# A hybrid attention and state-space trunk on one core: the two state-space stages become one, and the scanned states are laid by step, part and group

## What is computed

```python
proj = hn @ w_in;  u, z = proj[..., :1024], proj[..., 1024:]      # 64 groups of 16 channels
# per group, per direction, 64 complex states h:
#   h[t] = A * h[t-1] + B u[t],   y[t] = Re(C h[t])               (diagonal A)
y = (y_fwd + y_bwd) + d * u
gl = gelu(y);  y = gl * sigmoid(gl @ w_glu + b_glu);  y = y * silu(z)
return y @ w_out
```

## Time and profile before

| what | us |
|---|---|
| median of 3 runs (2629.58 to 2637.1) | 2631.95 |
| the profiled execution, its own time | 2628.88 |
| its span in the trace | 2627.0 |
| PE busy | 2325.1 |
| DVE busy | 1185.6 |
| ACT busy | 886.2 |
| POOL busy | 841.2 |

### The profile page before, as it was taken

How to read it: one execution, slowest core, us unless ns; L and a number is a source line. 1 busy time by engine, 2 the same in 40 slices (tenths; PEclk the granted TensorE clock), 3 DMA queues, 4 the chain that set the end, 5 groups by cost and what they waited for, 6 DMA issues and landing times. The chain is left out here.

```text
span 2627.0 us, 38336 instructions
## 1 busy us (share of the span) xinstructions
PE 2325.1 (89%) x13896; PEld 1865.8 (71%) x13896; DVE 1185.6 (45%) x2668; ACT 886.2 (34%) x2256; POOL 841.2 (32%) x1283
## 2 busy tenths in 40 slices
PE   4999999999999999999999999398799980558888
PEld 3777777777777777777777777277788760457767
DVE  5242443443353353353353353343325999435434
ACT  4233434333433433333333333232433210133221
POOL 1715655555565465466111111010111110211200
PEclk9999999999999999999999999599899995778989
DMA  4212221322222222222221220254554420874333
GB/s 143 60 51 61 60 80 51 84 74 56 74 67 73 66 75 73 66 83 65 64 63 45 47 63 21 65 185 155 202 169 150 144 93 0 213 208 154 136 138 120
DMA packets 191828, 249.69 MB, mean 95 GB/s; under 512 B 86176, under 2 KB 140320, under 8 KB 189472
## 3 DMA queue, kind: packets, MB, share of 16 engines
q1 hardware_dynamic: 191648, 247.30, 31.8%
HBM read 153.23 MB, written 62.55 MB: 82 GB/s over the span
## 5 line engine op out<-in xcount | busy, mean ns | idle before, releaser
L1066 PE MATMUL att_pj<-hT_hi,att_wh 128*128 128x512 f32 (+1 forms) x1920 | 710.0, 370 | 10.8 <-DVE att_wl L848 10.8
L1066 PE MATMUL att_pj<-hT_hi,att_wl 128*128 128x512 f32 (+1 forms) x1920 | 683.8, 356 | 0.0
L1066 PE MATMUL att_pj<-hT_lo,att_wh 128*128 128x512 f32 (+1 forms) x1920 | 682.7, 356 | 0.0
L704 POOL TENSOR_TENSOR att_sw<-att_sw,att_rope 128x1280 f32<-128x1280 f32 x48 | 201.5, 4198 | 762.9 <-DMA att_sw<-att_t 762.8
L1066 PEld LDWEIGHTS att_pj<-hT_hi,att_wh 128*128 128x128 f32 x1920 | 364.5, 190 | 58.5 <-DVE att_wl L848 11.4
L860 DVE CUSTOM_DVE_ANT_0 att_sm<-att_sc,att_mask 128x128 f32<-128x128 f32 (+2 forms) x480 | 152.4, 355 | 561.6 <-PE att_sc L982 560.4
L1066 PEld LDWEIGHTS att_pj<-hT_hi,att_wl 128*128 128x128 f32 x1920 | 363.6, 189 | 53.0
L1066 PEld LDWEIGHTS att_pj<-hT_lo,att_wh 128*128 128x128 f32 x1920 | 364.9, 190 | 45.5
L730 ACT ACTIVATE att_pr<-att_sm,att_stats 128x128 f32<-128x128 f32 (+2 forms) x480 | 215.0, 449 | 434.1 <-PE att_tr L992 313.0
L772 ACT COPY att_t<-att_pj 128x512 f32<-128x512 f32 (+1 forms) x216 | 111.3, 515 | 377.9 <-PE att_pj L1066 377.7
L879 DVE TENSOR_TENSOR att_t<-att_t,att_rope 128x1280 f32<-128x1280 f32 x48 | 71.8, 1495 | 201.8 <-DMA att_sw<-att_t 201.8
(11 more groups left out here) (224 smaller groups left out, 3835.7 us busy)
## 6 DMA issues: line engine op xcount, KB each, us to landing
att_raw<-in_w_att_dram SPq DMA_DIRECT2D x80, 512.0 KB, 3.8
att_sw<-att_t SPq DMA_DIRECT2D x192, 160.0 KB, 2.9
f_scratch<-att_ft SPq DMA_DIRECT2D x32, 256.0 KB, 2.3
e_scratch<-att_place SPq DMA_DIRECT2D x8, 1024.0 KB, 4.6
front_raw<-in_w_ssm_dram SPq DMA_DIRECT2D x16, 512.0 KB, 6.4
front_f<-f_scratch SPq DMA_DIRECT2D x16, 512.0 KB, 5.1
front_f<-e_scratch SPq DMA_DIRECT2D x16, 512.0 KB, 3.6
back_e<-e_scratch SPq DMA_DIRECT2D x8, 1024.0 KB, 7.5
```

Of the source, the lines that this page charges most:

```text
L704: pool.tensor_tensor(sw[:], sw[:], rope[:, 1], ALU.mult).then_inc(sin_done, 1)
L1066: last = pe.matmul(pj[:, c % 3, 0:n], w[:, k % 2, kt], h[:, kt, lo:lo + n], start=(r == 0), stop=(r == CHUNK_MMS - 1))
```

## The change

- The two stages become one (`ssm_stage`): no stage end stands between scan and back part. The SBUF of the front's weights and inputs is used again for the back part's matrices: the near matrices of all 64 groups at once (`near`), `e` in seven buffers, u and y in two. All eight PSUM banks serve the back part.
- The back part goes by 24 joints of 3, 3 and 2 groups per batch; the groups of a joint share a PSUM bank and one gelu. The near products of eight joints are made first (`near_part`); then, per joint, the two products with the entering states, and the near products of the joint seven ahead.
- Loads for the back part are issued when PE has finished the front's products, in the order near (8 transfers of 192 KB), u of two batches, two e, near (16 transfers), five e, then u of the third batch once the near products of the first are made.
- The forward half of the entering states is copied by ACT (`entering`) in place of POOL, the backward half still by DVE.
- `st` is laid by chunk, part, group: a scan step's 128 elements lie side by side, and one group's chunks 128 floats apart. `dec`, `t1`, `t2` follow. There is no zero column any more: column n holds the state that enters chunk n, so that the last chunk's leaving state is dropped and the scan has 31 and 96 steps.
- `leaving` of tile n-1 stands between c1 and c2 of tile n, where it stood after c2. ACT copies a group's forward half with one instruction of 318 elements, where it used two of 256 and 64; DVE's two become 254 and 62.

The core of the diff:

```diff
-        st = held.enter_context(nc.sbuf_tensor("states", [P, SG, 2, SCOLS], F32))
+        st = m.sb("states", [P, NC, 2, SG])
+        states = st[:].rearrange("p n r g -> p g r n")
...
+        e = m.sb("e", [P, E_BUFS, 2, GB, L * SC])
+        near = m.sb("near", [P, SG, P])
...
+            def u_again(b):
+                if b >= 2:
+                    sp.wait_ge(local, PARTS * (b - 1))
+                sp.dma_start(u2[:, b % 2], u_scratch[b].rearrange("s c g n -> (s c) g n")).then_inc(u2_in[b % 2], 16)
...
             sp.wait_ge(k_stored, 16 * HALVES)
+            sp.wait_ge(done, 3 * NT)
+            near_load(0)
+            u_again(0)
+            u_again(1)
+            for b in range(2):
+                e_load(b)
+            near_load(1)
+            near_load(2)
+            for b in range(2, E_BUFS):
+                e_load(b)
+            sp.wait_ge(stored, U_STORED)
+            u_again(2)
+            u_again(3)
...
+                    if c == len(CHUNKS) - 1 and 1 <= n <= NB:
+                        for g in range(GB * (n - 1), GB * n):
+                            act.wait_ge(left, g + 1)
+                            act.copy(states[0:64, g, :, 1:NC], part(g, slice(0, 64))[:, :, 0:NC - 1]).then_inc(fwd, 1)
                     act.wait_ge(done, 3 * n + c + 1)
...
+            def entering(j):
+                if j >= 2:
+                    act.wait_ge(y_done, j - 1)
+                g = joint_groups(j)
+                act.copy(en[0:64, j % 2, 0:len(g)], states[0:64, g[0]:g[-1] + 1]).then_inc(enter_f, 1)
...
-                prev = st[:, :, :, bass.ds(c, n, step=PC + 1)]
-                cur = st[:, :, :, bass.ds(c + 1, n, step=PC + 1)]
+                prev = st[:, bass.ds(c, n, step=PC)]
+                cur = st[:, bass.ds(c + 1, n, step=PC)]
...
                 for c, (lo, cnt) in enumerate(CHUNKS):
+                    if c == len(CHUNKS) - 1 and 1 <= n <= NB:
+                        leaving(n - 1)
...
-                if 1 <= n <= NB:
-                    leaving(n - 1)
...
+            for j in range(BANKS):
+                near_part(j)
+            for j in range(JOINTS):
+                b = j // PARTS
+                if j % PARTS == 0:
+                    pe.wait_ge(e_in[b], 16)
+                pe.wait_ge(enter_f, j + 1)
+                pe.wait_ge(enter_b, 2 * (j + 1))
...
+                last.then_inc(y_done, 1)
+                if j >= 1 and j - 1 + BANKS < JOINTS:
+                    pe.wait_ge(y_out, j)
+                    near_part(j - 1 + BANKS)
```

More of the change, by code:

```diff
@@ L59 @@
 NB = SG // GB
-SCOLS = NC + 2
 TWO_PI = 6.283185307179586
@@ L1279, with joint_groups, ssm_stage @@
 TAPS = 2 * L - 1
[L1282 to L1283 removed]
+BANKS = 8
+PART = 3
+PARTS = -(-GB // PART)
+JOINTS = NB * PARTS
+def joint_groups(j):
+    b, i = divmod(j, PARTS)
+    return list(range(GB * b + PART * i, min(GB * b + PART * (i + 1), GB * (b + 1))))
+def ssm_stage(nc, w_d, h_scratch, skip_d, f_scratch, e_scratch, bb_scratch, c0_scratch, decay_scratch,
+              u_scratch, z_scratch, kernel_scratch, y_scratch):
     NT = 2 * KT
@@ L1428, in _ @@
                                  [:, :, 0:(L - 1) * SC]).then_inc(k_out, 1)
-                if 1 <= n <= NB:
[L1430 to L1434, removed]
+            def entering(j):
[3 more added lines that the diff above has]
+                act.copy(en[0:64, j % 2, 0:len(g)], states[0:64, g[0]:g[-1] + 1]).then_inc(enter_f, 1)
+            act.wait_ge(stored, U_STORED)
+            act.wait_ge(k_stored, 16 * HALVES)
+            act.wait_ge(step, 4 * STEPS_ALL + 1)
+            entering(0)
+            entering(1)
+            for j in range(JOINTS):
+                b, g = j // PARTS, joint_groups(j)
+                act.wait_ge(y_done, j + 1)
+                if b >= 2 and j % PARTS == 0:
+                    act.wait_ge(y_stored[b % 2], 16 * L * (b // 2))
+                act.activation(yb[:, b % 2, g[0] % GB:g[-1] % GB + 1],
+                               py[:, j % BANKS, 0:len(g) * NC].rearrange("p (g n) -> p g n", n=NC),
+                               ACT.Gelu_apprx_tanh).then_inc(y_out, 1)
+                if j + 2 < JOINTS:
+                    entering(j + 2)
         @block.gpsimd
@@ new lines, in near_part @@
+            def near_part(j):
+                b = j // PARTS
+                if j % PARTS == 0:
+                    pe.wait_ge(u2_in[b % 2], 16 * (b // 2 + 1))
+                    for x, (lo, hi) in enumerate(NEAR_LOADS):
+                        if b == lo:
+                            pe.wait_ge(near_in[x], 16 * L)
+                for x, g in enumerate(joint_groups(j)):
+                    last = pe.matmul(py[:, j % BANKS, x * NC:(x + 1) * NC], near[:, g], u2[:, b % 2, g % GB],
+                                     start=(x == 0), stop=False)
+                last.then_inc(local, 1)
@@ new lines, in _ @@
+            pe.wait_ge(out, 3 * NT)
+            pe.wait_ge(k_out, 2 * HALVES)
+            for j in range(BANKS):
+                near_part(j)
+            for j in range(JOINTS):
+                b = j // PARTS
+                if j % PARTS == 0:
+                    pe.wait_ge(e_in[b], 16)
+                pe.wait_ge(enter_f, j + 1)
+                pe.wait_ge(enter_b, 2 * (j + 1))
+                groups = joint_groups(j)
+                for x, g in enumerate(groups):
+                    for ri in range(2):
+                        last = pe.matmul(py[:, j % BANKS, x * NC:(x + 1) * NC], e[:, b % E_BUFS, ri, g % GB],
+                                         en[:, j % 2, x, ri], start=False,
+                                         stop=(ri == 1 and g == groups[-1]))
+                last.then_inc(y_done, 1)
+                if j >= 1 and j - 1 + BANKS < JOINTS:
+                    pe.wait_ge(y_out, j)
+                    near_part(j - 1 + BANKS)
```

217 lines of the change are left out of this document (91 added, 126 removed).

## The result

| | us |
|---|---|
| the kernel before, median of 4 runs (2629.58 to 2637.10) | 2632.44 |
| the changed kernel, median of 4 runs (2590.91 to 2600.48) | 2595.67 |
| ratio, 95% interval | 0.9859 (0.9834 to 0.9883) |
| the profiled execution of the changed kernel, its span | 2590.91, 2589.1 |

The account below looks back on a forecast made before the run. Scan and back-stage loads stood in line; afterwards loads would bound joint 0 at 2212. Adding 54 gave the last gelu at 2266, GLU 6.0 later at 2272 against 2337.7 (-65.5): 2567 us, range 2542 to 2600.

Parts of the forecast that it names:

- the prediction's own sign: Stated sign of being wrong: joint 0 starting after 2225 means that the loads are slower than forecast.
- the rival with slower loads: Near loads go four ports at a time: joint 0 at 2235, time 2590; chance 0.08.
- Loads of the back part: Between PE's last front products (2167) and joint 0: u 5.6, e 17.7, near 17 us; joint 0 at 2212.
- two ends: Near's time in the back part's loads: 24.1 us at 174 GB/s or 10.1 at e's rate; middle taken, 17.
- The rival "slower still": Near loads slower still, four ports at a time: joint 0 at 2235, 2590 us; chance 0.08.
- Leaving states: Leaving states between c1 and c2: eight waits for u's reload, +9 us; taps about +1; -2.9 for the scan's start.
- the sum: Last gelu 2212 + 54 = 2266, GLU 6.0 us later at 2272 against 2337.7: -65.5 us, forecast 2567.
- Evictions: Copies into the new layout: ACT 0.72 us, DVE about 0.8 per group; no cost per tile, last eight 2 us later.
- Scan: DVE's scan: products 0.288 us, step 1.06, double step 1.56; 163 us instead of 230.6, end at 2185.5.
- Joints: Back part's joints: ACT sets the pace at 6.8 us per batch; 52.5 us, plus 1.6 for the first joint.
- Tail: From the last gelu's end to GLU: 6.0 us, as in the kernel before.

Follow-up runs that it names:

- the second trace: The changed kernel run once more, unaltered, for a second set of times and a second trace: median 2589.60 us, ratio 0.9854 to the kernel before.

## Why the prediction was right or wrong

The mechanism that the prediction put in bold held: the loads bound the start of the joints, not the scan. What failed is the size of one term, and with it the prediction's own sign came true (joint 0 after 2225). The range held the time only because it reached to the rival with slower loads.

- **Loads of the back part: the step that failed.** Near was put at 17 us and took 40. "For near I have two ends: 174 gives 24.1, e's rate 10.1 ... I take the middle, 17." From the first near load to the landing of the third u (PE goes on at 2238.01) were 64.5 us, not 43. With u and e, 9.3 MB, at 414 (22.4 us) and 2 us of start, 40 are left for near: 105 GB/s. The slower of the two ends was no bound: the 174 of the earlier trace rows came with 64 KB transfers in turn to eight ranges (158 in the run that does so here), and these are larger. Over all 128 partitions the same bytes in the same 512-byte pieces went at 302, so it is the reach that they lack. Joint 0 started at 2241.3 instead of 2212, and 21.5 of the 27 us that GLU's start missed are this. The rival "slower still" had the mechanism and nearly its place (2235); its chance of 0.08 was too low, since the argument against it, 174 in the window, was taken from transfers of another size. The Trainium skill, "SBUF — State Buffer", section "Door 1: The DMA port swizzle", gives 104 GB/s for 16 partitions; the whole near load agrees with 105, and the near windows of the two traces moved 110 to 122, a little above the page's figure.
- **Leaving states: right in kind, too small.** Forecast +9 for the waits and +1 for the taps; the order cost 11.9 (10.3 in the second trace) and 2.5. Near started at 2173.55, 6.5 us later than the 2167 of the sum: 4.4 of it are this, the other 2.1 stand in the kernel with leaving behind c2 too (2159.07 for the 2157 that the sum started from). The move gained nothing for the scan either: behind c2 it started at 2015.6, here at 2024.65 (forecast 2022.5).
- **Evictions: right.** 0.72 us on ACT, 0.86 on DVE (0.598 + 0.261) for 0.72 and 0.8. They cost PE nothing per tile, as reckoned: with leaving behind c2 its leaving products span 131.2 us, as in the kernel before (1881.6 to 2012.8).
- **Scan: right.** Products 0.29 for 0.288, step 1.10 for 1.06, double step 1.59 for 1.56; 170.9 us for 163. By the Trainium skill, "VectorE: DVE Perf Modes", section "Mode 1× (REGULAR) — the baseline", one result per cycle for any stride, the layout would do nothing; the run with the old layout shows 0.38 against 0.29 and contradicts it.
- **Joints: right in sum, wrong on who sets the pace.** 51.6 us (2241.3 to the last gelu's end, 2292.87) for 54. Copies of 960 took 1.85 for 1.96; no gelu waited for y's stores, as reckoned. But PE was as full as ACT, 44.98 and 43.25 of 55 us, and until 2280 it was ACT that waited for PE, 0.69 us in each batch. With quick copies (old layout) the joints were only 1.3 us faster (49.5 us between first and last joint for 50.8). The sum also took off 3.3 us for the two copies made before, where two copies of 960 are 3.9 at its own price.
- **Tail: right.** 5.9 us from the last gelu to GLU, 6.0 forecast.
- By the sum: 6.5 (late loads) + 21.5 (loads) + 1.3 (joint 0 after its u: twelve near products at the granted clock of 0.50, 1.2 GHz, took 3.29 us for the 2 of the sum) - 2.4 (joints) = 26.9; GLU started 26.8 us after the forecast 2272.

## To carry to other kernels

Before a bound is taken away, price what becomes the bound in its stead in the form that it will have there: here a rate read from 64 KB transfers (174) did not hold for 192 KB ones to the same 16 partitions (110 to 122). A matrix that would be loaded piece by piece into small partition ranges is better loaded over all partitions, even at the price of storing it several times where that is hidden: here it was worth 16 to 30 us. A scan 57 us shorter was worth 6 to 12 us while the loads bound the start; only with loads and leaving states mended did the joints start with the scan's end, 55 us earlier than in the changed kernel.

## What the hardware showed that I had not expected

- The DMA share is 1.26 to 1.31 in the windows of near, which move 110 to 122 GB/s, and 1.00 at 414: a full share is not a full rate.
- Issuing a transfer can hold the engine that issues: 16 near loads took SP 32.3 us, the longest single issue 9.55, and everything behind them in its program came later. On ACT twelve took 24.8. Two loads of the same bytes held SP 12.33 us in 512-byte pieces and 1.23 in long rows, so it is not the bytes alone that hold it. That it is the number of pieces is likely, but not shown.
- 512-byte pieces over 128 partitions went at 302 GB/s; with rows of 8 to 12 KB a window of all loads moved 421.
